# The first two output blocks of each projection computed together, x block by x block, and four PSUM banks for the queries and keys

## The reference

```
for l in range(DEPTH):
    x = x + 0.5 * swiglu(rmsnorm(x, ffn1_norm[l]), ffn1_wg[l], ffn1_wu[l], ffn1_wd[l])
    h = rmsnorm(x, mix_norm[l])
    x = x + (even_mixer(h, ...) if l % 2 == 0 else odd_mixer(h, ...))
    x = x + 0.5 * swiglu(rmsnorm(x, ffn2_norm[l]), ffn2_wg[l], ffn2_wu[l], ffn2_wd[l])
return rmsnorm(x, final_norm)
```

## Time and profile before

| | before |
|---|---|
| median of 3 runs | 2061.62 us (2060.53 to 2062.73) |
| span of the profiled execution | 2062.5 us |
| mean granted TensorE clock | 0.982 |
| PE busy | 1952.7 us, 95% |
| PEld, DVE, ACT, POOL busy | 77%, 48%, 34%, 16% |
| HBM | 173.85 MB read, 85 GB/s over the span |

### The profile page before, as it was taken

How to read it: one execution, slowest core, us unless ns; L and a number is a source line. 1 busy time by engine, 2 the same in 40 slices (tenths; PEclk the granted TensorE clock), 3 DMA queues, 4 the chain that set the end, 5 groups by cost and what they waited for, 6 DMA issues and landing times.

```text
span 2062.5 us, 23191 instructions
## 1 busy us (share of the span) xinstructions
PE 1952.7 (95%) x8888; PEld 1592.7 (77%) x8888; DVE 997.9 (48%) x1058; ACT 706.1 (34%) x932; POOL 334.4 (16%) x274
## 2 busy tenths in 40 slices
PE   6999999997989999999999999999948999999997
PEld 4888888785868888888878888887726778888885
DVE  6334421668778533342163343216988753433223
ACT  4222221436346422221142222214746542222212
POOL 2111100213113211110021111002345221111001
PEclk9999999998989999999999999999979999999998
DMA  4222222221211222222222222222210022222221
GB/s 148 99 102 100 83 102 102 96 78 37 82 42 42 92 92 102 102 88 95 102 82 102 102 93 90 102 102 90 82 41 21 22 82 102 94 89 102 102 102 41
DMA packets 36211, 176.66 MB, mean 86 GB/s; under 512 B 12752, under 2 KB 13136, under 8 KB 15552
## 3 DMA queue, kind: packets, MB, share of 16 engines
q1 hardware_dynamic: 33696, 172.55, 24.1%
q10 hardware_dynamic: 2304, 2.98, 0.4%
q0 software_dynamic: 160, 0.43, 0.1%
HBM read 173.85 MB, written 2.10 MB: 85 GB/s over the span
## 4 chain that ended last, share of the span: by engine, by line
PE 83%; DVE 8%; ACT 4%; POOL 2%; issue 2%; ACTq 0%; DMA 0%; POOLq 0%; DVEq 0%
PE ps L264 27%; PE ps L266 27%; PE ps L265 27%; POOL acc L333 2%; DVE xgl L299 1%; DVE eD L1180 1%; ACT eD L1135 1%; DVE small L1164 1%; DVE wl L234 1%; ACT wh L230 1%; DVE small L679 1%; DVE th L1755 1%; ACT eA L687 0%; PE ps L862 0%; DVE x L289 0%
## 5 line engine op out<-in xcount | busy, mean ns | idle before, releaser
L264 PE MATMUL ps<-xgh,wh 128*128 128x512 f32 x1792 | 709.9, 396 | 27.7 <-DVE xgl L299 25.4
L265 PE MATMUL ps<-xgl,wh 128*128 128x512 f32 x1792 | 698.8, 390 | 0.0
L266 PE MATMUL ps<-xgh,wl 128*128 128x512 f32 x1792 | 698.8, 390 | 0.0
L234 DVE TENSOR_TENSOR wl<-raw,wh 128x2048 fp32r<-128x2048 f32 (+1 forms) x157 | 360.3, 2295 | 541.1 <-ACT wh L230 541.0
L230 ACT ACTIVATE wh<-raw 128x2048 fp32r<-128x2048 f32 (+1 forms) x157 | 297.9, 1897 | 384.1 <-PE ps L266 382.8
L264 PEld LDWEIGHTS ps<-xgh,wh 128*128 128x128 f32 x1792 | 336.9, 188 | 110.9 <-DVE xgl L299 19.2
L265 PEld LDWEIGHTS ps<-xgl,wh 128*128 128x128 f32 x1792 | 337.0, 188 | 71.0 <-issue 3.4
L266 PEld LDWEIGHTS ps<-xgh,wl 128*128 128x128 f32 x1792 | 336.8, 188 | 71.1
L264 PE MATMUL ps<-ah,wh 128*128 (+1 forms) x704 | 273.9, 389 | 0.0
L265 PE MATMUL ps<-al,wh 128*128 (+1 forms) x704 | 273.9, 389 | 0.0
L266 PE MATMUL ps<-ah,wl 128*128 (+1 forms) x704 | 273.9, 389 | 0.0
(11 more groups left out here) (243 smaller groups left out, 1573.9 us busy)
## 6 DMA issues: line engine op xcount, KB each, us to landing
raw<-in_units SPq DMA_DIRECT2D x161, 1024.0 KB, 4.7
x<-in_xT ACTq DMA_DIRECT2D x8, 256.0 KB, 6.0
outT<-x SPq DMA_DIRECT2D x8, 256.0 KB, 2.1
relb<-in_rpb SPq DMA_DIRECT2D x64, 24.0 KB, 2.1
cosA<-in_rope_a ACTq DMA_DIRECT2D x1, 256.0 KB, 2.7
sinA<-in_rope_a ACTq DMA_DIRECT2D x1, 256.0 KB, 2.9
cosD<-in_rope_d POOLq DMA_DIRECT2D x1, 192.0 KB, 3.0
sinD<-in_rope_d POOLq DMA_DIRECT2D x1, 192.0 KB, 2.7
```

Source lines behind the costliest of these rows:

```text
L234: nc.vector.tensor_tensor(wl[:, c % 2, 0:n], raw[:, c % 2, 0:n], wh[:, c % 2, 0:n].bitcast(F32), ALU.subtract).then_inc(w_lo, 1)
L264: nc.tensor.matmul(dst, lh, rh, start=first, stop=False)
L265: nc.tensor.matmul(dst, lh, rl, start=False, stop=False)
L266: return nc.tensor.matmul(dst, ll, rh, start=False, stop=last)
```

## The change

`block_T2` computes both output blocks of a stage's first unit: for each x block it waits once and then issues three matmuls into one bank and three into another. It is used in `ffn_up_pe` for pair 0, in `even_pe` and in `odd_pe`. The norm matmul is issued behind both blocks instead of between them. In the even mixer the query and key blocks use banks 0, 1, 6 and 7 in turn (`qa_bank`) instead of 0 and 1, block i waits for `q32` of block i-4, and the rotation behind block i is that of block i-2; the last two rotations of these, 5 and 6, stand together behind block 7, and the reading of `rB` by tiny matmuls moves from behind block 1 to behind block 3.

```diff
+        def block_T2(pe, dsts, c, wait_x):
+
+            s = c % 2
+            for k in range(KD):
+                pe.wait_ge(xg_lo, wait_x + k + 1)
+                for m in range(2):
+                    o = k * 256 + m * P
+                    mm = three(dsts[m], wh[:, s, o:o + P], wl[:, s, o:o + P],
+                               xgh[:, k, :], xgl[:, k, :], k == 0, k == KD - 1)
+                    if k == KD - 1:
+                        mm.then_inc(w_half, 1)
...
         def ffn_up_pe(pe, f, B, n, p):
...
-            if not first:
+            if first:
+                block_T2(pe, (ps[:, 0, :], ps[:, 1, :]), c0, 8 * n)
+                norm_pe(pe, n, 4)
+            else:
                 pe.wait_ge(tg_done, 2 * p + 22 * f)
-            for m in range(2):
-                block_T(pe, ps[:, m, :], c0, m, wait_x=8 * n if first and m == 0 else None).then_inc(w_half, 1)
-                if first and m == 0:
-                    norm_pe(pe, n, 4)
+                for m in range(2):
+                    block_T(pe, ps[:, m, :], c0, m).then_inc(w_half, 1)
...
+        def qa_bank(i):
+
+            return (0, 1, 6, 7)[i % 4]
...
         def even_pe(pe):
-            for i in range(8):
+            pe.wait_ge(w_lo, BE + 1)
+            block_T2(pe, (ps[:, qa_bank(0), :], ps[:, qa_bank(1), :]), BE, 8)
+            norm_pe(pe, 1, 4)
+            pe.wait_ge(even_in, 64)
+            for i in range(2, 8):
                 c = BE + i // 2
                 pe.wait_ge(w_lo, c + 1)
-                if i >= 2:
-                    pe.wait_ge(q32_done, i - 1)
-                block_T(pe, ps[:, i % 2, :], c, i % 2, wait_x=8 if i == 0 else None).then_inc(w_half, 1)
-                if i == 0:
-                    norm_pe(pe, 1, 4)
-                    pe.wait_ge(even_in, 64)
-                else:
-                    rot_pe(pe, i - 1)
-                if i == 1:
+                if i >= 4:
+                    pe.wait_ge(q32_done, i - 3)
+                block_T(pe, ps[:, qa_bank(i), :], c, i % 2).then_inc(w_half, 1)
+                if i == 3:
                     norm_reads_pe(pe)
+                rot_pe(pe, i - 2)
+            rot_pe(pe, 6)
...
         def odd_pe(pe):
-            odd_block_pe(pe, 0)
+            pe.wait_ge(w_lo, BO + 1)
+            block_T2(pe, (ps[:, 0, :], ps[:, 1, :]), BO, 32)
             norm_pe(pe, 4, 4)
-            for i in range(1, 8):
+            for i in range(2, 8):
                 odd_block_pe(pe, i)
```

More of the change, by code:

```diff
@@ L266, in three, with block_T @@
             return nc.tensor.matmul(dst, ll, rh, start=False, stop=last)
-        def block_T(pe, dst, c, m, width=P, step=256, nt=KD, wait_x=None):
+        def block_T(pe, dst, c, m, width=P, step=256, nt=KD):
             s = c % 2
             for k in range(nt):
-                if wait_x is not None:
-                    pe.wait_ge(xg_lo, wait_x + k + 1)
                 o = k * step + m * P
@@ L1268, in even_pe @@
                         pe.wait_ge(rcol_read, 1)
+                    if v == 0 and t >= 2:
+                        pe.wait_ge(q32_done, t + 5)
                     if v == 1:
@@ L1384, in even_dve @@
                     dve.wait_ge(qc_done, i - 1)
-                nc.vector.tensor_tensor(q32[:, i % 2, :], ps[:, i % 2, :], rB[:, :], ALU.mult).then_inc(q32_done, 1)
+                nc.vector.tensor_tensor(q32[:, i % 2, :], ps[:, qa_bank(i), :], rB[:, :], ALU.mult).then_inc(q32_done, 1)
                 if i >= 1:
@@ L1500, in odd_block_pe @@
                 pe.wait_ge(cstd_done, i - 7)
-            block_T(pe, ps[0:rows, i % 4, :], c, m, width=rows,
-                    wait_x=32 if i == 0 else None).then_inc(w_half, 1)
+            block_T(pe, ps[0:rows, i % 4, :], c, m, width=rows).then_inc(w_half, 1)
         def odd_pe(pe):
-            odd_block_pe(pe, 0)
+            pe.wait_ge(w_lo, BO + 1)
+            block_T2(pe, (ps[:, 0, :], ps[:, 1, :]), BO, 32)
             norm_pe(pe, 4, 4)
-            for i in range(1, 8):
+            for i in range(2, 8):
                 odd_block_pe(pe, i)
```

## The result

| | before | changed |
|---|---|---|
| median | 2061.62 us (2059.53 to 2064.56, 5 runs) | 2050.34 us (2048.20 to 2055.76, 5 runs) |
| span of the profiled execution | 2062.5 us | 2046.4 us |
| PE busy | 1952.7 us | 1944.1 us |

The changed kernel takes 0.9945 of the time before, interval 0.9931 to 0.9960, some 11.3 us less. The two profiled executions differ by more, 16.1 us, because the one of the changed kernel is the shortest of its five, and its clock was better.

The account below looks back on a forecast made before the run. Matmuls on PE were taken to bound the kernel, 1952.7 of 2062.5 us. Terms 3 x 3.03 + 1.15 + 1.8 - 1.8 = 10.2 us, off 2061.6, gave 2051.4 us, with 2048.8 to 2055.0 for 8 in 10.

Parts of the forecast that it names:

- The gain per start: Starts of third and last feed-forward and odd mixer gain 3.03 us each, second feed-forward 1.15, as PE's x waits go.
- The norm's slack of 0.4 us: Feed-forward starts: the 11.4 us chain from norm matmul to next unit fits before PE needs it, by about 0.4 us.
- The second rival: VectorE and GpSimd slow each other, so PE waits at feed-forward starts and in the even mixer; 2055 to 2057, chance 0.12.
- First start: First feed-forward: no gain, PE waits about 4 us for `wl`, the clock falls; 1.8 us lost, bounds 0 and 2.5.
- first rival: The clock does not fall at the first start: 1.8 us better, 2049.6 us; chance 0.17.
- Even mixer: Of 3.03 us about 1.8 is left, bounds 0.8 and 2.5, because the chain behind each rotation now binds.
- The three new waits: Even mixer: PE waits 0.8 us at block 2, 0.9 after rotation 3, and 1.5 at rotation 6 for `q32`.
- The reads of `rB`: Even mixer, after block 3: PE's norm reads, put at 1.6 us, come before rotation 1.
- the chain from a rotation to the next unit's `wl`: Even mixer: from a rotation until the next unit is ready, 7.7 us with PE's own start.
- Sum: Whole kernel: all terms together gain 10.2 us, from 2061.6 to 2051.4 us; forecast's chance 0.63.

Follow-up runs that it names:

- the repeat: The changed kernel unaltered, run again for a second profile: median 2052.27 us, ratio 0.9945 [0.9932, 0.9959] to the kernel before.

## Why the prediction was right, point by point

The forecast was 2051.4, measured were 2050.3 and 2052.3. That the total fits within some 1 us is partly luck: the ten executions of this kernel spread from 2048.2 to 2055.8, and the stage lengths add up to 1.5 us more gain than forecast.

**The gain per start** (3.03, 1.15): right, 3.1 and 3.1 in the third and last feed-forward, 1.1 in the second. What made it fit is that the loss was counted as a block's excess over its 24 matmuls at the steady pace, not as the sum of its listed waits. The odd mixer gave 3.3: from the stage's first row to the wait of the earlier trace rows the gain is 3.1 (54.81 us before; that matmul now starts at 1450.30, 51.71 us behind), and another 0.2 comes in the stretch behind. Its cause stays open; differences of that size are found between profiles of one order: 269.4 to 270.0 us in the four kernels with the old order in this stage, 265.7 to 266.4 in seven of the eight with the pair (267.8 in the one with the norm matmul later).

**The norm's slack of 0.4 us**: right, 0.49 was measured. The chain took 11.3 us where 11.4 had been added up (without the 0.16 us from the root's end to the reciprocal's start in the earlier trace rows), and one block more of delay turned it into a wait at all four feed-forwards. The second rival, that VectorE and GpSimd slow each other there and the slack is gone, did not come about.

**First start** (-1.8, bounds 0 and 2.5): right in kind. The wait was foreseen as about 4 us that ends at 33.1; it was 2.89 and 3.88 us, ending at 32.6. The clock fell in the repeat (1.5 us lost), in the kernel with the feed-forwards alone (1.7) and in the one with two banks (2.8, beyond the bound), not in the first profile of the changed kernel. So forecast and first rival are both true, each in some executions.

**Even mixer** (1.8, bounds 0.8 and 2.5): the mechanism was right and the size too small. Up to the scores 2.6 was measured, just beyond the bound, and up to V, for which the 1.8 was worked out, 2.8. The three new waits were put at 0.8, 0.9 and 1.5 us and came as 0.9, 0.6 and 1.2. PE, in the changed kernel:

```profile
393.70 0.47 PE L264 MATMUL ps<-xgh,wh 128*128 128x512 f32 x1 [0.92 <-DVE wl L234]
...
399.24 1.02 PE L671 MATMUL ps<-q,permA 128*128 128x512 f32 x2
...
405.68 1.05 PE L645 MATMUL ps<-ones,rB 1*128 1x1 f32 x8
406.65 1.13 PE L671 MATMUL ps<-q,permA 128*128 128x512 f32 x2
...
413.09 1.02 PE L671 MATMUL ps<-q,permA 128*128 128x512 f32 x2
...
420.49 0.50 PE L264 MATMUL ps<-xgh,wh 128*128 128x512 f32 x1
...
426.06 1.02 PE L671 MATMUL ps<-q,permA 128*128 128x512 f32 x2
...
434.06 1.13 PE L671 MATMUL ps<-q,permA 128*128 128x512 f32 x2 [0.63 <-DVE q L1403]
434.62 0.68 PE L264 MATMUL ps<-wh,xgh 128*128 128x256 f32 x1
```

The stage starts 0.51 us earlier here, its first matmul too. Rotation 0 came when it was forecast (399.24 + 0.5 = 399.7), block 4 had no wait, and block 6 did start late behind rotation 3 (1.05 us from one to the other, where it is 0.45 without a wait) and rotation 6 waited, as worked out. Two terms were too large. The reads of `rB` were put at 1.6 us and took 0.97, so rotation 2 came 0.4 early. The 1.6 was a misreading of the earlier trace rows. Before, PE's reads came at

```profile
399.16 1.05 PE L634 MATMUL ps<-ones,rB 1*128 1x1 f32 x8
```

and lasted until 400.14, so they took 0.98 us then too; the rest belonged to rotation 0, which behind its wait took 1.06 us (398.10 to 399.16) where a rotation takes 0.46 otherwise. And the chain from a rotation to the next unit's `wl` was put at 7.7 us from the earlier trace rows; it is 7.4 here (413.09 to 420.49), and as much less behind rotation 4. Together the terms make the 1.0 us by which V came earlier than forecast. In that chain one link differs. The sum of sine and cosine parts, behind rotation 2, is

```profile
414.94 0.69 DVE L1485 TENSOR_TENSOR qs<-qs,qc 128x512 f32<-128x512 f32 x1
```

and before the change, behind the same rotation at 412.10 and with GpSimd's cosine product beside it:

```profile
413.07 1.30 POOL L1479 TENSOR_TENSOR qc<-q,cosA 128x512 f32<-128x512 f32 x1 [5.05 <-DVE q L1385]
```

```profile
413.16 0.69 DVE L1464 TENSOR_TENSOR qs<-ps,sinA 128x512 f32<-128x512 f32 x1 [0.17 <-PE ps L656]
...
413.95 0.96 DVE L1467 TENSOR_TENSOR qs<-qs,qc 128x512 f32<-128x512 f32 x1
```

The product runs until 414.37, and the sum that starts meanwhile ends 0.54 us after it. After the change the rotation comes a block later, the product is long done, and the sum is not delayed. The sine product, whose one operand comes from PSUM, runs beside the same GpSimd operation in its usual 0.69. The Trainium skill, page "SBUF — State Buffer", section "SBUF: two separate sides", says that VectorE with two SBUF inputs and a GpSimd operation that reads SBUF exclude each other for the whole instruction. The trace agrees in all three rows: the sum is held up by the product, the operation with an operand in PSUM is not. This is read from rows; no run here separates it from the rest.

**Sum.** Forecast 10.2; stage by stage 11.7 with the clock's fall at the first start, 13.2 without; medians 11.3. The 0.8 us too little in the even mixer is the largest error of a term. One thing was left out of the sum altogether: behind the old order's wait of 1.1 us in the even mixer the clock fell in two of four profiles, and against those the change gains another 1.7 us. So the forecast compared with the old kernel's better case, the one that its profile happened to show.

## What to carry to other kernels

Measure a stall by what the block takes over its matmuls at the steady pace, not by its listed waits (at the third feed-forward 2.0 us were listed and 3.1 were to be had). Where a pair of blocks shares one wait, ask at each place what else PE will now want earlier: at the first start this was a weight split that stood behind setup work, and moving the setup made a kernel of 2044.8 us out of one of 2050 to 2052, though the same move alone is worth nothing. A chain that fits with 0.5 us to spare is worth leaving where it is: one block later, each feed-forward lost 6.7 to 10.0 us. One profile of a kernel is one case of its clock: take a second one before a microsecond is put down to an edit.

The best kernel measured is the changed one with the setup behind pair 0 and the early split in the even mixer, 2044.25 us, 0.9916 [0.9902, 0.9929] of the time before; the early split's share in that is within the noise.

## What the runs showed of the hardware that was not expected

- Behind the same wait the clock falls in one execution and not in another. Over the twelve profiles: behind the even mixer's wait of 1.1 us it fell in two of four, behind the odd mixer's wait of 1.9 us in nine of twelve (not in the kernel with the odd mixer's pair alone, in the repeat and in the one with only the setup moved on top of the change), behind the first start's wait of 2.89 us it did not, and behind those of 3.69, 3.78, 3.86 and 3.88 us it did, as behind all five of 4.8 to 5.0 us in the kernels with the later norm and with two banks. At the first start this makes 1.5 to 2.8 us between executions.
- The mean clock in the attention behind the scores was 0.94, 0.95 or 0.96 over some 220 us, for the same instructions, and the stretch took up to 3.9 us longer at 0.94 than at 0.96, more than a whole start is worth.
- A VectorE sum of two SBUF operands took 0.69 us alone and 0.96 to 1.22 us where GpSimd's product of 1.3 us had already begun.
